# No alignment padding ahead of the expert loop, and two norms on 512 tokens done in two halves

## What is computed

```python
def rms_norm(x, w):
    xf = x.astype(jnp.float32)
    y = xf * lax.rsqrt(jnp.mean(xf * xf, axis=-1, keepdims=True) + EPS)
    return (y * w.astype(jnp.float32)).astype(x.dtype)
...
        x = x + g1 * rms_norm(y_lat, norm_post_mix[l])
        h_lat = rms_norm(x, norm_pre_ffn[l]) * (1.0 + sc2) + sh2
        x = x + g2 * rms_norm(conv_ffn(h_lat, ...), norm_post_ffn[l])
        if with_ctx_out:
            ctx = ctx + g1c * rms_norm(y_ctx, norm_post_mix[l])
            h_ctx = rms_norm(ctx, norm_pre_ffn[l]) * (1.0 + sc2c) + sh2c
            ctx = ctx + g2c * rms_norm(conv_ffn(h_ctx, ...), norm_post_ffn[l])
```

## Time and profile before

| what | value |
|---|---|
| median of 3 runs | 3585.29 us |
| lowest and highest | 3583.42 and 3586.99 us |
| the profiled execution's own time | 3587.29 us |
| its span | 3585.5 us |
| TensorE matmuls busy | 3414.7 us (95% of the span) |
| VectorE, ScalarE busy | 774.9 us (22%), 678.8 us (19%) |
| granted TensorE clock, mean over the span | 0.962 of full |
| instructions | 76230 |

### The profile page before, as it was taken

The page is one execution under the profiler, slowest core; times in us unless marked ns, Lnnn a source line. Parts: engine busy times, 40 slices in busy tenths (PEclk is TensorE's granted clock), DMA queues, the critical chain, the costliest instruction groups (busy, mean ns, idle before and its releaser), DMA issues.

```text
span 3585.5 us, 76230 instructions
## 1 busy us (share of the span) xinstructions
PE 3414.7 (95%) x32714; PEld 2830.7 (79%) x32715; DVE 774.9 (22%) x1802; ACT 678.8 (19%) x1469; POOL 92.8 (3%) x141
## 2 busy tenths in 40 slices
PE   8999799999999999999999999969999999999998
PEld 4456658874566788887888887759999999988898
DVE  1214636650103221213210113220100100011001
ACT  2224122220204331212110112201111211110011
POOL 0000000110001010100000010000000000000000
PEclk9999689999899999999999999979999999999999
DMA  6446012222223243333343443328999999954477
GB/s 270 176 153 235 3 47 87 89 67 73 77 94 124 96 152 129 132 120 112 128 147 134 146 142 106 106 71 346 362 358 369 361 370 350 369 180 152 139 268 272
DMA packets 94764, 637.63 MB, mean 178 GB/s; under 512 B 10784, under 2 KB 11824, under 8 KB 38592
## 3 DMA queue, kind: packets, MB, share of 16 engines
q1 hardware_dynamic: 92048, 627.58, 48.0%
q0 software_dynamic: 2608, 8.49, 0.7%
HBM read 634.98 MB, written 1.05 MB: 177 GB/s over the span
## 4 chain that ended last, share of the span: by engine, by line
PE 92%; DVE 3%; ACT 2%; DMA 2%; issue 1%; SPq 0%; DVEq 0%; ACTq 0%
PE bank L528 24%; PE bank L950 20%; PE bank L620 18%; PE bank L571 7%; PE bank L640 5%; PE bank L542 4%; PE bank L907 2%; PE bank L476 1%; PE bank L502 1%; PE bank L676 1%; PE bank L965 1%; PE bank L658 1%; PE bank L665 1%; DMA ring<-in_moe_down 1%; PE bank L1017 1%
## 5 line engine op out<-in xcount | busy, mean ns | idle before, releaser
L528 PE MATMUL bank<-H,ring 128*128 128x256 f32 (+1 forms) x3040 | 774.0, 416 | 6.9 <-ACT H L1125 6.1
L528 PEld LDWEIGHTS bank<-H,ring 128*128 128x128 f32 x3040 | 580.1, 192 | 184.6 <-issue 112.0
L620 PE MATMUL bank<-PROJ,ring 128*64 128x96 f32 (+2 forms) x7776 | 667.5, 282 | 12.3 <-ACT SC L1174 9.6
L620 PEld LDWEIGHTS bank<-PROJ,ring 128*64 128x64 f32 (+1 forms) x7776 | 547.3, 147 | 131.2 <-issue 97.4
L950 PE MATMUL bank<-MIX,ring 128*64 128x96 f32 x12544 | 523.5, 247 | 9.9 <-issue 9.9
L950 PEld LDWEIGHTS bank<-MIX,ring 128*64 128x64 f32 x12544 | 522.1, 138 | 12.0 <-issue 11.8
L1878 DVE TENSOR_TENSOR PROJ<-SC,bank 128x96 f32 (+2 forms) x246 | 70.8, 288 | 624.5 <-ACT SC L1315 620.3
L950 PE MATMUL bank<-H,ring 128*128 128x256 f32 x896 | 193.7, 379 | 0.0
L950 PEld LDWEIGHTS bank<-H,ring 128*128 128x128 f32 x896 | 170.2, 190 | 23.4 <-issue 0.3
L640 PE MATMUL bank<-H,ring 128*128 128x256 f32 x768 | 176.7, 387 | 3.9 <-ACT PROJ L1196 3.7
L640 PEld LDWEIGHTS bank<-H,ring 128*128 128x128 f32 x768 | 147.1, 194 | 27.8 <-issue 7.9
(11 more groups left out here) (314 smaller groups left out, 2715.3 us busy)
## 6 DMA issues: line engine op xcount, KB each, us to landing
ring<-in_moe_up SPq DMA_DIRECT2D x224, 1024.0 KB, 5.3
ring<-in_moe_down SPq DMA_DIRECT2D x128, 896.0 KB, 6.1
ring<-in_up SPq DMA_DIRECT2D x44, 1024.0 KB, 4.8
ring<-in_mod_b SPq DMA_DIRECT2D x40, 1024.0 KB, 5.7
ring<-in_tproj SPq DMA_DIRECT2D x32, 1024.0 KB, 4.9
ring<-in_proj SPq DMA_DIRECT2D x26, 1024.0 KB, 4.8
ring<-in_gates SPq DMA_DIRECT2D x24, 1024.0 KB, 4.9
ring<-in_down SPq DMA_DIRECT2D x32, 704.0 KB, 4.1
```

What stands on the lines that cost most here:

```text
L528: mm = pe.matmul(B[(tile + t) % 4][:, 0:width], w[:, k, t * P:(t + 1) * P], src[:, k, 0:width], start=k == 0, stop=k == k_n - 1)
L620: mm = pe.matmul(B[bank][lo:lo + m, 0:width], w[:, k, lo:lo + m], src(s * half + k), start=s == 0 and k == 0, stop=s == 1 and k == half - 1)
```

## The change

The directive ahead of the expert loop is taken out. Norms 1 with 2 and 3 with 4 change as follows: the residual runs over the latent halves of all eight tiles and then over the context halves (32 operations in place of 16); the squares of norms 2 and 4 follow in the same order, 16 of half the columns; TensorE sums the latent half into bank 7 and the context half into bank 6; there are two roots, two reciprocals and two broadcasts (banks 4 and 5); VectorE multiplies and ScalarE shifts the latent half first and the context half after it. On each engine the order is fixed: TensorE has both halves' means ahead of both broadcasts, and both broadcasts ahead of the next product; ScalarE has the first half's root behind the second half's squares; VectorE has the second half's reciprocal behind the first half's eight multiplications. The products behind the norms wait for the latent half first and for the context half where they use it. One counter (`norm_sq`) replaces those of single norms, and `NORM_AT` and `SQ_AT` say where each norm stands in the counters.

```diff
+        NORM_AT = {n: i + 1 for i, n in enumerate(n for n in range(13) if n not in (2, 4))}
+        SQ_AT = {n: KT * (n + (n > 2) + (n > 4)) for n in range(13)}
...
+            def norm_by_half(n, at):
+
+                for s in range(2):
+                    for k in range(KT):
+                        pe.wait_ge(S("norm_sq"), SQ_AT[n] + s * KT + k + 1)
+                        for c in range(2):
+                            cols = slice(s * T + c * P, s * T + (c + 1) * P)
+                            mm = pe.matmul(B[7 - s][:, c:c + 1], H[:, k, cols], mean_d[:, 0:1], start=k == 0 and c == 0, stop=k == KT - 1,
+                                           skip_group_check=True)
+                    mm.then_inc(S("half_ms"), 1)
+                for s in range(2):
+                    pe.wait_ge(S("half_r"), at + s + 1)
+                    for c in range(2):
+                        mm = pe.matmul(B[4 + s][:, c * P:(c + 1) * P], stat[:, 2 * s + c:2 * s + c + 1].to_broadcast([P, P]), ident,
+                                       start=True, stop=True)
+                    mm.then_inc(S("half_b"), 1)
...
-                    product(w_quarter(u, 0, 0), x_quarter(0, 0, n), 0, 0, (ready, per, per) if first else None)\
+                    product(w_quarter(u, 0, 0), x_quarter(0, 0, n), 0, 0, (ready, 1, 1) if first else None)\
                         .then_inc(S("sv_p1"), 1)
-                    product(w_quarter(u, 0, 1), x_quarter(1, 0, n), 1, 0, (ready, 5 * per, per) if first else None)
+                    product(w_quarter(u, 0, 1), x_quarter(1, 0, n), 1, 0, (ready, 5, 1) if first else None)
...
                     if first:
+                        pe.wait_ge(S(ready), KT * per)
...
 
                 pe.wait_ge(S("mo_sel"), 1)
                 gather()
-                pe.addr_align(256)
                 with pe.Fori(0, N_EXPERTS) as e:
...
             norm(1, TC, 2)
-            norm(2, TC, 0)
+            norm_by_half(2, 0)
...
             norm(3, TC, 3)
-            norm(4, TC, 0)
+            norm_by_half(4, 2)
...
             for j in range(4):
-                fm_unit(u0 + j, t0 + 2 * j, H, T, ready=("norm4_out", 0, 2) if j == 0 else None)
+                fm_unit(u0 + j, t0 + 2 * j, H, T, ready=("norm4_out", 0, 1) if j == 0 else None)
+            pe.wait_ge(S("norm4_out"), 2 * KT)
...
-                act.wait_ge(S("norm_ms"), n + 1)
+                act.wait_ge(S("norm_ms"), NORM_AT[n])
...
+            def squares_by_half(n, sem):
+
+                for s in range(2):
+                    for k in range(KT):
+                        act.wait_ge(S(sem), s * KT + k + 1)
+                        act.activation(H[:, k, s * T:(s + 1) * T], X[:, k, s * T:(s + 1) * T], ACT.Square).then_inc(S("norm_sq"), 1)
+                    if s == 1:
+                        roots_by_half(n, 0)
+                roots_by_half(n, 1)
+
+            def roots_by_half(n, s):
+                act.wait_ge(S("half_ms"), (n // 2 - 1) * 2 + s + 1)
+                act.activation(stat[:, 2 * s:2 * s + 2], B[7 - s][:, 0:2], ACT.Sqrt, bias=eps).then_inc(S("half_rt"), 1)
+
+            def shift_by_half(n, row, sh, l):
+
+                for s in range(2):
+                    for k in range(KT):
+                        act.wait_ge(S(f"norm{n}_scaled"), s * KT + k + 1)
+                        part = H[:, k, s * T:(s + 1) * T]
+                        act.activation(part, part, ACT.Identity, bias=MOD[:, l, sh + k, s:s + 1], scale=AB[:, row, k, s:s + 1])\
+                           .then_inc(S(f"norm{n}_out"), 1)
...
-            squares(2, X, TC, S("norm1_out"), 1, 1)
-            root(2, TC)
-            shift(2, 2, 24, TC, 0)
+            squares_by_half(2, "norm1_out")
+            shift_by_half(2, 2, 24, 0)
...
-            squares(4, X, TC, S("norm3_out"), 1, 1)
-            root(4, TC)
+            squares_by_half(4, "norm3_out")
             act.wait_ge(S("mod_ready"), 2)
-            shift(4, 0, 0, TC, 1)
+            shift_by_half(4, 0, 0, 1)
...
+            def modulate_by_half(n, at):
+
+                for s in range(2):
+                    dve.wait_ge(S("half_rt"), at + s + 1)
+                    dve.reciprocal(stat[:, 2 * s:2 * s + 2], stat[:, 2 * s:2 * s + 2]).then_inc(S("half_r"), 1)
+                    dve.wait_ge(S("half_b"), at + s + 1)
+                    for k in range(KT):
+                        cols = slice(s * T, (s + 1) * T)
+                        dve.tensor_tensor(H[:, k, cols], X[:, k, cols], B[4 + s][:, 0:T], ALU.mult).then_inc(S(f"norm{n}_scaled"), 1)
+
+            def residual_by_half(n):
+
+                for k in range(1, KT - 1):
+                    sum_square(n, k, TC)
+                recip_root(n, TC)
+                for i in range(2 * KT + 1):
+                    if i < 2 * KT:
+                        k, cols = i % KT, slice(i // KT * T, (i // KT + 1) * T)
+                        dve.tensor_tensor(Y[:, k, cols], Y[:, k, cols], B[4][:, cols], ALU.mult).then_inc(S(f"norm{n}_scaled"), 1)
+                    if i > 0:
+                        k, cols = (i - 1) % KT, slice((i - 1) // KT * T, ((i - 1) // KT + 1) * T)
+                        dve.wait_ge(S(f"norm{n}_scaled"), i)
+                        dve.tensor_tensor(X[:, k, cols], X[:, k, cols], Y[:, k, cols], ALU.add).then_inc(S(f"norm{n}_out"), 1)
...
-                    dve.wait_ge(S("norm3_out"), KT)
+                    dve.wait_ge(S("norm3_out"), 2 * KT)
...
-                dve.wait_ge(S(ready), 4 * (width // T))
+                dve.wait_ge(S(ready), KT + 4)
...
-            residual(1, TC)
+            residual_by_half(1)
             w_sums("up0", 0, 0)
             w_sums("up0", 1, 0)
-            modulate(2, TC)
+            modulate_by_half(2, 0)
...
-            residual(3, TC)
+            residual_by_half(3)
             mod_factors(1, 0, 4)
-            modulate(4, TC)
+            modulate_by_half(4, 2)
...
-            pool.wait_ge(S("norm_ms"), 4)
+            pool.wait_ge(S("norm_ms"), NORM_AT[3])
```

More of the change, by code:

```diff
@@ L482, in norm @@
                     means(0, True, False)
-                    pe.wait_ge(S(f"norm{n}_sq"), KT)
+                    pe.wait_ge(S("norm_sq"), SQ_AT[n] + KT)
                     means(KT - 1, False, True).then_inc(S("norm_ms"), 1)
@@ L486, in norm @@
                     for k in range(KT):
-                        pe.wait_ge(S(f"norm{n}_sq"), k + 1)
+                        pe.wait_ge(S("norm_sq"), SQ_AT[n] + k + 1)
                         mm = means(k, k == 0, k == KT - 1)
                     mm.then_inc(S("norm_ms"), 1)
-                pe.wait_ge(S("norm_r"), n + 1)
+                pe.wait_ge(S("norm_r"), NORM_AT[n])
                 for c in range(width // P):
@@ L1108, in squares @@
                     act.wait_ge(sem, first + every * k)
-                    act.activation(H[:, k, 0:width], src[:, k, 0:width], ACT.Square).then_inc(S(f"norm{n}_sq"), 1)
+                    act.activation(H[:, k, 0:width], src[:, k, 0:width], ACT.Square).then_inc(S("norm_sq"), 1)
             def root(n, width):
-                act.wait_ge(S("norm_ms"), n + 1)
+                act.wait_ge(S("norm_ms"), NORM_AT[n])
                 act.activation(stat[:, 0:width // P], B[7][:, 0:width // P], ACT.Sqrt, bias=eps).then_inc(S("norm_rt"), 1)
+            def squares_by_half(n, sem):
[16 more added lines that the diff above has]
+                           .then_inc(S(f"norm{n}_out"), 1)
             def sqrt_table(src):
@@ L1132, in take_tile @@
             def take_tile(n, k, bank, row, width):
-                act.activation(H[:, k, 0:width], bank[:, 0:width], ACT.Square).then_inc(S(f"norm{n}_sq"), 1)
+                act.activation(H[:, k, 0:width], bank[:, 0:width], ACT.Square).then_inc(S("norm_sq"), 1)
                 for s in range(width // T):
@@ L1473, in sum_square @@
             def sum_square(n, k, width):
-                dve.wait_ge(S(f"norm{n}_sq"), k + 1)
+                dve.wait_ge(S("norm_sq"), SQ_AT[n] + k + 1)
                 ins = dve.tensor_tensor(H[:, 0, 0:width], H[:, 0, 0:width], H[:, k, 0:width], ALU.add)
@@ L1482, in recip_root @@
             def recip_root(n, width):
-                dve.wait_ge(S("norm_rt"), n + 1)
+                dve.wait_ge(S("norm_rt"), NORM_AT[n])
                 dve.reciprocal(stat[:, 0:width // P], stat[:, 0:width // P]).then_inc(S("norm_r"), 1)
-                dve.wait_ge(S("norm_b"), n + 1)
+                dve.wait_ge(S("norm_b"), NORM_AT[n])
             def modulate(n, width):
```

## The result

| | before | changed |
|---|---|---|
| median | 3586.14 us (4 runs) | 3555.72 us (4 runs) |
| lowest and highest | 3583.42 and 3587.75 | 3554.98 and 3569.74 |
| ratio, 95% interval | | 0.9925, 0.990 to 0.995 |
| the profiled execution's time, span | 3587.29, 3585.5 | 3569.74, 3567.9 |
| mean granted clock, profiled execution | 0.962 | 0.963 |

The kernel is faster by 30 us in the medians (18 to 36 us by the ratio's interval), where 21 were forecast; 3555.7 lies just under the range of 3558 to 3571. The one execution that was profiled is also the slowest of its four, and it gained 17.55 us against the profiled one of before. So two questions are open: whether each part gave what was forecast, and what separates a gain of 17.5 us from one of 30.

The account below looks back on a forecast made before the run. TensorE, carrying 92% of the span, was taken as the bound. Loop entry -17.1, norm 2 -1.7 and norm 4 -2.6 sum to -21.4 us off the median 3585.3: 3564 us, range 3558 to 3571.

Parts of the forecast that it names:

- The entry: Gather to first expert product: without the 226 NOPs that product starts at 2402.15 in place of 2419.30, -17.1 us.
- Rival A: At the loop's entry, the branch of line 982 still waits for code: 3567.5 us; chance 0.13.
- D: Padding was hidden: ScalarE's or VectorE's loop entry holds the products anyway, only the norms gain: 3581 us; chance 0.04.
- Norm 2: Norm pair ahead of up0: with halves, up0's first two products end at 528.9 in place of 530.66, -1.7 us.
- Norm 4: Norm pair ahead of proj1: with halves, proj1's first tile ends at 982.4 in place of 985.0, -2.6 us.
- E: The norms give nothing and the loop's entry gives all: 3568 us; chance 0.07.
- The clock's return at the entry: First expert's products: full clock may return sooner after a shorter stop; taken as 0, at most 2.7 us gained.
- rival B: The clock returns sooner at the loop's entry or in a norm: 3561 us; chance 0.12.
- off the median: Whole kernel: the sum of -21.4 us was subtracted from the median of 3585.3 us, giving 3563.9.
- between: Stretch from the twelfth of norm 6's means matmuls to the gather, untouched by the change: forecast 0.
- theory S: Later stages' half-clock time depends on their start against clock changes; six added products: untouched stages lose 2 to 5 us.
- Rival C: Expert loop not staying loaded, if its head lies above slot 166: two blocks reloaded per return, 50 us, 3614; chance 0.04.

Follow-up runs that it names:

- e1: The changed kernel once more, with no edit: 3556.96 us, ratio 0.9923.
- e2: The kernel before without the alignment line, nothing else changed: 3570.66 us, ratio 0.9964.
- e4: The kernel before with the loop's head kept on a block boundary, the padding branched over instead of executed: 3569.31 us, ratio 0.9963.
- e6: The changed kernel with the loop's head put on slot 200 of a 256-instruction block, the gap branched over: 3649.44 us, ratio 1.0172.
- e7: The changed kernel with norms 3 and 4 whole again, only norms 1 and 2 in halves, no padding: 3561.5 us, ratio 0.993.
- e8: The changed kernel with norm 4's first broadcast among the second half's means, its second behind proj1's first unit, first root earlier: 3555.0 us, ratio 0.9917.
- e10: The kernel before without the alignment line, plus six unneeded float32 products in proj1's second unit: 3571.49 us, ratio 0.9958.
- e11: e8's kernel with norm 2's first broadcast also moved among its second half's means and weight sums reordered: 3552.62 us, ratio 0.9909.
- e12: The changed kernel with the loop's head put on slot 140 of a 256-instruction block, the gap branched over: 3560.11 us, ratio 0.9925.
- e9: The kernel before without the alignment line, plus three unneeded float32 products in proj1's second unit: 3568.86 us, ratio 0.9952.
- e3: The changed kernel with the alignment line put back, so only the norms in halves: 3577.71 us, ratio 0.9979.
- e5: The kernel before once more, with no edit, for a second profile: 3587.72 us.

## Why the prediction was right, and where it failed

**The entry** was right to 0.3 us in nine of eleven profiles without executed padding: -17.1 forecast, -16.8 to -17.2 in e1, e2, e4, e6, e7, e8, e10, e11 and e12. Two profiles gave less, the first one, -15.7, and e9, -15.5, because the gather ran at half clock (6.97 and 7.03 us, 5.63 before). The 1.92 us of the eighth turn was the right row for the head's price: 2.04 was measured, 2.20 in e1. That the branch would be quick was right too. The reading of why was half right: e3 and e5 confirm that a branch into a block just after a boundary can wait for code (2.30 and 2.12 us), but e4 shows that it costs nothing when the head is entered early enough. Rival A is excluded by the longest branch, 0.37 us, D by the entry itself.

**The norms** were right in mechanism and near in size. Norm 2: -1.7 forecast, -1.9 to -2.4 measured. Here one reading was wrong: 530.66 in the earlier trace rows is the second product's last matmuls (`bank<-H,ring`), and up0's third product (`bank<-H,VT`) began at 531.20. Its forecast start, 528.9, was right: the first profile has 530.25 with norm 1 begun 1.4 us later than before, so 528.8. Against 531.20 the same steps give -2.3. Norm 4: -2.6 forecast, -2.1 and -2.8 in two profiles of the same kernel, -3.8 in e12; from its first means matmul to the first tile's end 24.8 and 24.1 us, 24.3 forecast. e7 shows norm 4's share by itself, and e2 that both are zero without the halves. E is excluded by the rows of both norms.

**The clock's return at the entry** is the term that was mis-sized. I put it at nothing with 2.7 us as its bound; it measured -1.0 in the first profile and -2.7, all of the bound, in e1; -1.7 to -2.6 in e2, e7, e8, e10, e11 and e12, -1.0 in e9 and nothing in e4. So rival B was right at the entry, in most profiles; in the norms it was wrong in both profiles of the changed kernel (23.9 us each), and held in norm 4 of e12, and of e8 and e11 with their moved broadcast (20.5 us).

**The step that failed** is the sum itself: "off the median" every stage outside the edits was held fixed. In e1 the stages from norm 6's means to the gather are 4.5 us shorter, in e7 3.1, in e8 8.4, in e11 and e12 9.3, at the same work. With e1's profile the account closes: 17.1 + 2.7 + 1.9 + 2.8 + 4.5 = 29.0 us, less 0.9 of scatter elsewhere, is 28.1. In the first profile "between" gave nothing and the other stages lost 3.6 us, which makes its 17.6; the three executions beside it have no trace, but their granted clock (0.968 to 0.969, against 0.963) says that they spent less time at the lower level; that this was "between" is likely by the other profiles and not shown. A thousandth of mean clock over 3560 us is 7 us at 1.2 GHz in place of 2.4, or 3.6 us of time, so 0.005 to 0.006 is 18 to 21 us by that rough measure, and 14 were measured.

**What stays open.** Shown is that a few microseconds of work added or taken away ahead of norm 5 go along with 0 to 9 us less in stages that are not touched, through the clock and not through waits. By the table behind e10 the amount goes with how far behind a fall of the clock norm 6's means stand. Not settled is whether that place is the cause, why e6 falls out of the order, and whether the two parts really gain more together than apart. The particular forecast of theory S for e10 failed.

**Rival C** had a threshold that lies between the tested slots 140 and 200, and the wrong price: 13.2 us per return in place of 7.2. With that price the risk was 92 us, not 50.

## What to carry to other kernels

Ahead of a loop, alignment by executed NOPs costs 0.073 us each on the engine that sets the time; ask of it whether the loop still fits the instruction memory from where it starts, count the blocks it spans, and reach a boundary, if one is wanted, by a branch. When a chain of norm steps runs across three engines, halve it, and then look at which engine's fixed order holds the first half back: here the first broadcast stood behind the second half's means; the new order was worth 1.0 us in norm 4 at the same clock, and the fastest version of all has it moved in both norms, though its 3 us lie within the intervals. On a kernel bound by TensorE, a saving of a few microseconds can come with as much again, or nothing, from the clock in stages behind it: compare busy time at equal matmul counts before giving such a difference a cause.

## What the runs showed of the hardware that was not expected

- The jump over the padding takes 0.70 us (e4), where 226 NOPs took 16.5.
- A late block of code has no fixed price: 3.82, 2.12 and 2.30 us for the same branch in the kernel before (twice) and in e3, and nothing in e4, where its load had about 4 us of cover.
- One block too many makes this loop reload all of its code: 145 packets in place of 81, with stops in up to four places per turn.
- The same 5182 to 5184 matmuls from norm 6's means to the gather are busy for 1119 to 1129 us in the fourteen profiles, by the clock. The row of e12, the shortest of them:

```profile
1212.14:2383.54 1171.40, 1119.24 (x5182) 959.26 (x5183) 258.62 (x689) 214.27 (x474) 42.87 (x78) 0.96 0.38 128
```
